# Issuing the weight pieces, raw mLSTM weights and their parts from ScalarE, with the pieces' maxima in the middle of VectorE's step

## The reference, cut to what matters

```python
h = rms_norm(x, p['norm1_w']) * (1.0 + sc1) + sh1
proj = h @ p['w_in']                       # rq, rk, rv, rg | mq, mk, mv, mo, mi, mf
q_r = rotary(_heads(rq, R_HEADS), pos)
k_r = rotary(_heads(rk, R_HEADS), pos) * (R_DK ** -0.5)
def step(S, inp):                          # retention, chunks of 128 tokens
    s = jnp.einsum('bhtd,bhsd->bhts', qc, kc) * inner
    o = einsum(s, vc) + jnp.einsum('bhtd,bhde->bhte', qc * qdec[..., None], S)
    S = cdec[:, None, None] * S + jnp.einsum('bhsd,bhse->bhde', kc * kdec[..., None], vc)
y_r = head_norm(_merge(o_r), p['ret_norm_w'], R_HEADS) * jax.nn.silu(rg)
```

## Time and profile before

| | before |
|---|---|
| time, median of 3 runs | 2862.22 us (2860.45 to 2865.99) |
| profiled execution | 2870.42 us, its span 2868.6 us |
| TensorE busy | 2580.2 us, 90% |
| VectorE busy | 1677.5 us, 58% |
| ScalarE busy | 793.4 us, 28% |
| GpSimd busy | 397.3 us, 14% |
| HBM traffic over the span | 97 GB/s |
| mean granted TensorE clock | 0.943 of full speed |

### The profile page before, as it was taken

The page is one execution under the profiler, slowest core; times in us unless marked ns, Lnnn a source line. Parts: engine busy times, 40 slices in busy tenths (PEclk is TensorE's granted clock), DMA queues, the critical chain, the costliest instruction groups (busy, mean ns, idle before and its releaser), DMA issues. The chain is left out here.

```text
span 2868.6 us, 44774 instructions
## 1 busy us (share of the span) xinstructions
PE 2580.2 (90%) x17400; PEld 1570.8 (55%) x17400; DVE 1677.5 (58%) x3305; ACT 793.4 (28%) x1145; POOL 397.3 (14%) x389
## 2 busy tenths in 40 slices
PE   7798777996988999769969999999999987999998
PEld 1254444555776787635535666666666652444444
DVE  2646666753676776737875767766667765222222
ACT  1222222220443544304442222222222224111110
POOL 0022212220000000001232222122222200000000
PEclk9899988996999999769989999999999998999999
DMA  9724444427102010043311111111111107332321
GB/s 327 211 91 169 140 170 176 172 71 245 33 23 85 27 58 24 20 140 130 132 66 45 61 60 56 57 41 59 57 57 59 60 31 257 93 104 69 104 69 46
DMA packets 192688, 279.31 MB, mean 97 GB/s; under 512 B 16017, under 2 KB 131265, under 8 KB 188755
## 3 DMA queue, kind: packets, MB, share of 16 engines
q1 hardware_dynamic: 192604, 278.19, 29.8%
HBM read 202.95 MB, written 75.21 MB: 97 GB/s over the span
## 5 line engine op out<-in xcount | busy, mean ns | idle before, releaser
L279 PE MATMUL d_po<-d_w,d_a_parts 128*128 128x512 f16 x704 | 268.6, 381 | 27.8 <-DVE d_w L2719 27.8
L280 PE MATMUL d_po<-d_w,d_a_parts 128*128 128x512 f16 x704 | 268.6, 382 | 0.0
L281 PE MATMUL d_po<-d_w,d_a_parts 128*128 128x512 f16 x704 | 268.4, 381 | 0.0
L2248 PE MATMUL py<-h_parts,wide_weights 128*128 128x384 f16 (+1 forms) x792 | 246.4, 311 | 17.9 <-DVE u_p L2384 17.9
L2249 PE MATMUL py<-h_parts,wide_weights 128*128 128x384 f16 (+1 forms) x792 | 246.2, 311 | 0.0
L2250 PE MATMUL py<-h_parts,wide_weights 128*128 128x384 f16 (+1 forms) x792 | 246.1, 311 | 0.0
L279 PE MATMUL prj<-w_heads,h_parts_t 128*128 128x512 f16 x512 | 197.7, 386 | 9.9 <-DVE h_parts_t L864 5.0
L280 PE MATMUL prj<-w_heads,h_parts_t 128*128 128x512 f16 x512 | 197.7, 386 | 0.0
L281 PE MATMUL prj<-w_heads,h_parts_t 128*128 128x512 f16 x512 | 197.2, 385 | 0.0
L279 PE MATMUL m_prj<-m_h,w_heads 128*128 128x128 f16 (+1 forms) x1088 | 179.2, 218 | 11.4 <-DMA m_h<-h_parts 10.1
L2706 DVE SCALAR_TENSOR_TENSOR d_out<-d_po,d_scale,g_p 128x1024 f32<-128x1024 f32 x16 | 20.5, 1284 | 287.5 <-PE d_po L281 287.5
(11 more groups left out here) (432 smaller groups left out, 5699.7 us busy)
## 6 DMA issues: line engine op xcount, KB each, us to landing
wa<-in_w_ada_dram SPq DMA_DIRECT2D x12, 2048.0 KB, 21.5
u_raw<-in_w_up_dram SPq DMA_DIRECT2D x44, 512.0 KB, 5.0
d_a<-act_cols SPq DMA_DIRECT2D x15, 1408.0 KB, 7.3
act_cols<-u_a SPq DMA_DIRECT2D x44, 384.0 KB, 2.4
win_raw<-in_w_in_dram SPq DMA_DIRECT2D x8, 2048.0 KB, 17.2
S_s<-in_w_up_dram SPq DMA_DIRECT2D x8, 1408.0 KB, 7.1
w_piece<-in_w_up_dram SPq DMA_DIRECT2D x8, 1408.0 KB, 8.6
d_raw<-in_w_down_dram SPq DMA_DIRECT2D x11, 1024.0 KB, 6.9
```

Source lines behind the costliest of these rows:

```text
L279: nc.tensor.matmul(out, left[0], right[0], start=(k == 0), stop=False)
L280: nc.tensor.matmul(out, left[0], right[1], start=False, stop=False)
L281: return nc.tensor.matmul(out, left[1], right[0], start=False, stop=last)
L2248: nc.tensor.matmul(out, left[0], right[0], start=(start and k == 0), stop=False, skip_group_check=True)
```

## The change

SP no longer issues the pieces, the store of the parts or the loads of raw blocks 1 to 3 (block 0 stays with it). ScalarE issues them: a pair of pieces behind each of its steps 1 to 12 (inside `load_pieces`, waiting for the maxima of the pair before), and the parts with the next raw block in the middle of steps 4, 6 and 8, behind `h_hi`; the last parts go in step 10. To place these, ScalarE's loop over steps 2 to 9 is partly written out. VectorE takes a pair's two maxima between `h_lo` and `state` of the same step 2 to 13 in which it took them at the end.

```diff
@@ sync
-            load_pieces(0, True)
             step(1)
             with sp.Fori(0, 3) as b:
                 step(2 * b + 2)
-                load_pieces(2 * b + 1)
                 loads(2 * b + 3)
-                prep.store_parts(sp, b)
-                prep.load_raw(sp, b + 1)
                 save_y(2 * b + 2, P)
-                load_pieces(2 * b + 2)
             step(8)
-            load_pieces(7)
             loads(9)
-            prep.store_parts(sp, 3)
             save_y(8, P)
-            for j in range(UPIECES, 3 * UPIECES // 2):
-                load_pieces(j)
-                step(j + 2)
+            with sp.Fori(10, NCH - 2) as c:
+                step(c)
@@ scalar
+            def load_pieces(of, at, j):
+
+                for u in range(2):
+                    if not isinstance(j, int) or j:
+                        act.wait_ge(s["piece_maxed"], 2 * j + u - 1)
+                    act.dma_start(piece[u], of[bass.ds(2 * at + u, 1)].rearrange("o p n -> (o p) n")).then_inc(s[f"piece_in{u}"], 16)
+
             norm.square(act, 2, P)
             step(1, P, P, P, P, qs_p)
-            with act.Fori(0, 4) as b:
-                step(2 * b + 2, P, P, P, P, qs_p)
+            load_pieces(up_pieces, 0, 0)
+            def next_weights(b):
+                prep.store_parts(act, b)
+                prep.load_raw(act, b + 1)
+
+            step(2, P, P, P, P, qs_p)
+            load_pieces(up_pieces, 1, 1)
+            step(3, P, P, P, P, qs_p, lambda: prep.cut_hi(act, 0))
+            load_pieces(up_pieces, 2, 2)
+            with act.Fori(1, 3) as b:
+                step(2 * b + 2, P, P, P, P, qs_p, lambda: next_weights(b - 1))
+                load_pieces(up_pieces, 2 * b + 1, 2 * b + 1)
                 step(2 * b + 3, P, P, P, P, qs_p, lambda: prep.cut_hi(act, b))
-            with act.Fori(10, NCH - 2) as c:
+                load_pieces(up_pieces, 2 * b + 2, 2 * b + 2)
+            step(8, P, P, P, P, qs_p, lambda: next_weights(2))
+            load_pieces(up_pieces, UPIECES - 1, UPIECES - 1)
+            step(9, P, P, P, P, qs_p, lambda: prep.cut_hi(act, 3))
+            load_pieces(down_pieces, 0, UPIECES)
+            step(10, P, P, P, P, qs_p, lambda: prep.store_parts(act, 3))
+            load_pieces(down_pieces, 1, 9)
+            with act.Fori(11, NCH - 3) as c:
                 step(c, P, P, P, P, qs_p)
+                load_pieces(down_pieces, c - 9, c - 1)
+            step(NCH - 3, P, P, P, P, qs_p)
@@ vector, step
                 if Tn:
                     h_lo(c + 1, Tn)
+                if pieces:
+                    find_max(c - 2)
                 state(c - 1)
@@ vector, loops
-                step(2 * b + 2, P, P, P, P, steps, mask_p, lambda: prep.find_scale(dve, b))
-                find_max(2 * b)
-                step(2 * b + 3, P, P, P, P, steps, mask_p, lambda: prep.cut_lo(dve, b))
-                find_max(2 * b + 1)
+                step(2 * b + 2, P, P, P, P, steps, mask_p, lambda: prep.find_scale(dve, b), True)
+                step(2 * b + 3, P, P, P, P, steps, mask_p, lambda: prep.cut_lo(dve, b), True)
-                step(c, P, P, P, P, steps, mask_p)
-                find_max(c - 2)
+                step(c, P, P, P, P, steps, mask_p, None, True)
```

More of the change, by code:

```diff
@@ L593, in _ @@
             norm.load_x(sp, x_rows[2], 2, P)
[L595 to L601, removed]
             def loads(c):
@@ L939, in find_max, with step @@
                     nc.vector.tensor_reduce(core.wmax[:, bass.ds(2 * j + u, 1)], piece[u], AX.X, ALU.max, apply_absolute_value=True).then_inc(s["piece_maxed"], 1)
-            def step(c, T, Ta, Tn, Tnn, steps, mask, between=None):
+            def step(c, T, Ta, Tn, Tnn, steps, mask, between=None, pieces=False):
                 rotate(c, T, steps)
```

## The result

| | before | after |
|---|---|---|
| time, median | 2862.12 us (2860.45 to 2865.99, 4 runs) | 2885.74 us (2883.18 to 2888.87, 4 runs) |
| ratio to before | | 1.0081, 95% interval 1.0064 to 1.0099 |
| profiled execution | 2870.42 us, span 2868.6 us | 2883.18 us, span 2881.3 us |
| TensorE busy | 2580.2 us | 2578.1 us |
| VectorE busy | 1677.5 us | 1689.7 us |

The kernel became 23.6 us slower.

A forecast was written before the change was run, and what follows sets the result against it. TensorE was taken to bound steps 10 to 13, VectorE's chain the even steps. 14.4 + 0 - 0.1 - 27.1 + 10 + 5 = +2.2 us gave 2864.4 us; forecast's own range 2857 to 2868, overall 2851 to 2878.

The forecast's parts named there:

- What bounds the kernel: Retention phase: TensorE bounds steps 10 to 13, VectorE's chain the even steps; odd steps take about 30 us.
- Steps 10 to 13, maxima ahead of the state, +14.4: State shifts 5.85 us, TensorE waits for y and x, steps become 29.9 us: +14.4 us.
- Odd steps, 0: Odd steps 3 to 9: state starts late anyway, maxima fill part of that wait, 29.9 us a step: 0.
- Step 2, -0.1: Step 2: scale's chain behind x shrinks to 20.1 us, step 36.4 against 36.5 us: -0.1 us.
- Steps 4, 6, 8, -27.1 and the raw block +10: Steps 4, 6, 8: waits for x and y vanish, -27.1 us; VectorE waits for late raw blocks, +10 us.
- ScalarE's own time, 0: ScalarE's issues and waits for maxima stay hidden before TensorE needs scaled q and k: 0, bound 1 us per step.
- The clock, +5: Steps 10 to 13: TensorE's clock may fall to half behind new waits, 0 to 6.8 us, taken as +5.
- The rivals: Slower by late raw block, 0.36; faster by clean transfers, 0.26, including 0.03 for TensorE not waiting in steps 10 to 13.
- The slower one: Late raw block at the reduction in steps 4, 6, 8, up to 18.4 us of waits; 2868 to 2884 us, chance 0.36.
- Two of the stated signs of being wrong: Signs included even steps over 42 us, raw block landing past 21 us, and steps 10 to 13 still at 26 us.

The follow-up runs named there:

- the exchange on GpSimd: Changed kernel with GpSimd's sine part of the next chunk ahead of the reduction over partitions in steps 2, 4, 6, 8: ratio 0.9982, 2860.9 us.
- the sine part held: Kernel before with both maxima ahead of the state in steps 10 to 13 only, GpSimd's sine part held until x is normalised: ratio 1.0053, 2883.9 us.
- another order of VectorE's work: Pieces, parts, raw blocks on ScalarE ahead of h_hi, with even-step maxima inside the scale's search: ratio 1.0003, 2867.5 us.

## Why the prediction was wrong, step by step

The forecast was +2.2 us and the time +23.6, past the range. In the order of its steps:

- **What bounds the kernel:** right for the odd steps and for 10 to 13. Wrong for the even ones: "from the scale's first reduction to the next H it is 26.06 us, all on VectorE's chain". GpSimd's chain (reduction, 7 us, sine part) ran beside the maxima and ended 1.2 us behind them: VectorE already waited for it.
- **Steps 10 to 13, maxima ahead of the state, +14.4:** the mechanism was right, the shift and the waits at both turns of TensorE came as worked out (1.1 us for y instead of 1.3). The term lacked 0.9 us a step for the norm of x, which the sine part slows from 0.75 to 1.74 us when it lands beside it.
- **Odd steps, 0:** right, 29.8 us against 29.9 forecast.
- **Step 2, -0.1:** this is the step that failed. It subtracted the maxima's 6.0 us from a chain of which they were not the bound (26.06 - 6.0 = 20.1; measured 25.66); step 2 grew by 5.25. The same was missed in steps 4, 6 and 8. In sum 21 us of the 24.2 by which the trace's +26.4 passes the forecast, and the exchange on GpSimd gave all of it back.
- **Steps 4, 6, 8, -27.1 and the raw block +10:** the waits for x and y went as forecast, and the raw block cost 6.6 us against 10 (it took 17.0 us in step 4 and 21.7 in step 6). With 3 x 5.25 us for the sine part that is -4.8; measured -4.5. The reason given was half right: the maxima do cover what x is late, but the pieces behind x gave at most 0.4 us of it. x was earlier since the store and the raw block were issued 11 us later.
- **ScalarE's own time, 0:** right; ScalarE scales k at 578.33 in step 12 with its waits and issues done by 574.2.
- **The clock, +5:** right in kind, 8.0 in size. It fell in all four steps, twice for about twice as long.
- **The rivals:** none held the cause. The slower one named the raw block, at 18.4 us of waits; it cost 6.6, less than even the forecast's +10, and the time passed the upper end of that case too (2884). Two of the stated signs of being wrong came: the even steps from 4 on took over 42 us, and the raw block of step 6 landed after 21.7.

So 26.4 us of the trace are 14.4 + 8.0 + 3.5 for steps 10 to 13, 21.0 for GpSimd in the four even steps, 6.6 for the raw block, and -27.1 for x and y.

## What to carry to other kernels

When an operation is moved away from a place, ask which other engine's latency it covered there: subtracting it from a chain is right only when the next release is checked on every engine that feeds the chain. An operation that is moved ahead costs nothing up to the slack of what stands behind it and everything beyond, and stalls of TensorE of 1.1 and 3.3 us in a step were paid a second time by its clock here, with 8.0 us in four steps. And a transfer gained little here by another queue alone or by an earlier issue behind the same weights alone; it gained by both together, or by the others being issued later.

## What the hardware did that I had not expected

- GpSimd starts its next elementwise operation 6.7 to 7.7 us behind a reduction over partitions, 9.5 to 9.8 in another order of VectorE's work, with nothing in the profile that it waits for.
- VectorE's norm of x (128 x 1024 float32) took 1.74 us beside GpSimd's sine part and 0.75 without, while the maxima took 3.08 us with or without company.
- TensorE's granted clock fell to the lower level behind waits of 1.1 and 2.3 us with 0.9 us of transposes between, in four steps of four with the sine part held. In the changed kernel it fell behind waits of 1.0 and 2.3 us in steps 2, 4 and 6 and stayed at 1.00 in step 8. It stayed at 1.00 behind 0.6 us in three steps and behind 1.6.
- Two queues moved x no sooner than one when it was issued at the same place (12.1 against 12.5 us); issued 4.7 us earlier, it landed after 12.5 us in a queue apart and after 16.3 in one queue.
